# Forget gate moved into the attention stage, weight slots shared across stages, paired transposes, TensorE code without loops

## The reference, cut to what matters

```python
def even_layer(x, g_norm, w_in, b_f, w_out):          # x: (1, 1024, 1024)
    z = rms_norm(x, g_norm) @ w_in
    qa, ka, va, ga, fa, qb, kb, vb, gb = jnp.split(z, cuts, axis=-1)   # fa: 16 columns, the others 1024
    log_f = jax.nn.log_sigmoid(fa.astype(f32) + b_f.astype(f32))
    ya = forgetting_attention(hA(qa), hA(ka), hA(va), log_f)           # 16 heads of 64
    yb = dilated_attention(hB(qb), hB(kb), hB(vb))                     # 16 heads of 64
    y = jnp.concatenate([ya * jax.nn.silu(ga), yb * jax.nn.silu(gb)], axis=-1)
    return x + y @ w_out

# forgetting_attention: c = cumsum(log_f) over the sequence;
#   s = q.k * scale + c[t] - c[s], causal;  p = softmax(s);  o = p @ v
```

## Time and profile before

| | us |
|---|---|
| median of 3 runs | 4086.0 (4082.72 to 4088.43) |
| the profiled execution | 4084.06 |
| its span, first to last instruction | 4082.3 |
| PE busy | 3702.8 (91%) |
| DVE, ACT, POOL busy | 1756.0, 1314.9, 1336.3 |
| mean granted TensorE clock | 0.946 of full speed |

### The profile page before, as it was taken

How to read it: one execution, slowest core, us unless ns; L and a number is a source line. 1 busy time by engine, 2 the same in 40 slices (tenths; PEclk the granted TensorE clock), 3 DMA queues, 4 the chain that set the end, 5 groups by cost and what they waited for, 6 DMA issues and landing times. The chain is left out here.

```text
span 4082.3 us, 49492 instructions
## 1 busy us (share of the span) xinstructions
PE 3702.8 (91%) x17232; PEld 2952.5 (72%) x17232; DVE 1756.0 (43%) x3204; ACT 1314.9 (32%) x2399; POOL 1336.3 (33%) x795
## 2 busy tenths in 40 slices
PE   5987687879999996699999999997898999999797
PEld 4776554668888885588888888886677676868486
DVE  4666433353333335256565565655313323242432
ACT  3777132121001112265555655555101202020210
POOL 3210200233333330355555556664322121312032
PEclk8997799889999998899999999998999999999998
DMA  3000101221111101211311212310512020211141
GB/s 93 21 6 6 45 20 54 88 62 47 51 42 50 51 31 57 58 53 49 49 51 52 37 34 38 36 36 6 181 47 98 26 66 21 67 39 54 44 162 67
DMA packets 216104, 213.71 MB, mean 52 GB/s; under 512 B 12464, under 2 KB 174512, under 8 KB 216000
## 3 DMA queue, kind: packets, MB, share of 16 engines
q1 hardware_dynamic: 194160, 153.11, 14.4%
q10 hardware_dynamic: 21840, 59.25, 4.0%
HBM read 178.72 MB, written 33.62 MB: 52 GB/s over the span
## 5 line engine op out<-in xcount | busy, mean ns | idle before, releaser
L1138 POOL TENSOR_SCALAR even_probs<-even_probs,even_stat 128x128 f32<-128x128 f32 (+7 forms) x256 | 442.2, 1734 | 329.1 <-DVE even_stat L1515 329.1
L502 PE MATMUL ps<-all_u_hi,even_w_hi 128*128 128x512 f32 x1024 | 425.9, 416 | 25.1 <-POOL even_w_lo L1130 25.1
L506 PE MATMUL ps<-all_u_hi,even_w_lo 128*128 128x512 f32 x1024 | 403.0, 394 | 0.0
L505 PE MATMUL ps<-all_u_lo,even_w_hi 128*128 128x512 f32 x1024 | 400.3, 391 | 0.0
L455 POOL CAST odd_w_hi<-odd_w_raw 128x1024 fp32r<-128x1024 f32 x80 | 89.1, 1114 | 896.7 <-PE ps L502 688.1
L1520 DVE TENSOR_TENSOR even_probsT_lo<-ps,even_probsT_hi 128x512 fp32r<-128x512 f32 (+3 forms) x384 | 213.0, 555 | 280.8 <-ACT even_probsT_hi L1369 279.4
L502 PE MATMUL ps<-all_u_hi,odd_w_hi 128*128 128x512 f32 x768 | 305.5, 398 | 5.7 <-DVE ret_yT L2524 3.7
L505 PE MATMUL ps<-all_u_lo,odd_w_hi 128*128 128x512 f32 x768 | 303.4, 395 | 0.0
L506 PE MATMUL ps<-all_u_hi,odd_w_lo 128*128 128x512 f32 x768 | 303.1, 395 | 0.0
L1360 ACT ACTIVATE even_probs<-even_probs,even_stat 128x128 f32<-128x128 f32 (+7 forms) x256 | 199.0, 778 | 313.1 <-DVE even_stat L1509 313.1
L502 PEld LDWEIGHTS ps<-all_u_hi,even_w_hi 128*128 128x128 f32 x1024 | 194.2, 190 | 59.8 <-POOL even_w_lo L1130 25.5
(11 more groups left out here) (405 smaller groups left out, 8521.3 us busy)
## 6 DMA issues: line engine op xcount, KB each, us to landing
even_w_raw<-in_even_w_in_dram SPq DMA_DIRECT2D x64, 512.0 KB, 6.6
odd_w_raw<-in_odd_w_in_dram SPq DMA_DIRECT2D x48, 512.0 KB, 3.8
mlp_w_raw<-in_w_up_dram SPq DMA_DIRECT2D x32, 512.0 KB, 4.0
mlp_w_raw<-in_w_down_dram SPq DMA_DIRECT2D x32, 512.0 KB, 3.6
scratch_h<-residual SPq DMA_DIRECT2D x2, 4096.0 KB, 17.2
even_bias<-scratch_negc ACTq DMA_DIRECT2D x16, 512.0 KB, 6.4
scratch_yt<-even_yT ACTq DMA_DIRECT2D x32, 256.0 KB, 2.0
we_y_raw<-scratch_yt ACTq DMA_DIRECT2D x16, 512.0 KB, 4.3
```

Source lines behind the costliest of these rows:

```text
L502: ins = nc.tensor.matmul(dst, lh, rh, start=first, stop=False)
L505: nc.tensor.matmul(dst, lh, rl, start=False, stop=False)
L506: return nc.tensor.matmul(dst, ll, rh, start=False, stop=last)
L1138: nc.gpsimd.tensor_scalar(PB[g % 2][:, at], PB[g % 2][:, at], inv[:, s:s + 1], None, ALU.mult)\
```

## The change

1. **Forget gate.** `forget_stage` is gone. Its weight is loaded by SP first thing in the even stage into idle buffers, split by POOL, and its 48 matmuls stand on PE between the fourth and the fifth half product of the first pair (PSUM banks 6 and 7). Its chain on ACT and DVE stands between the copies; ACT itself issues the store of the sums, waits for it after the v copies, and only then issues the two bias reads of the first pair, which stood at the head of the stage before.
2. **Weight slots.** One pair of slots (`kept`) lives from "wo" to the end; the MLP adds two to them. `ne` now loads and splits two weights, the first pair's q and k. At its end the even stage loads and splits the first two slots of "we".
3. **Turns two by two.** In every even step PE issues the turns of n and n+1 one after the other, then the scores, eighths and weighing of n, then those of n+1. ACT and DVE copy both in the even step. The ring has 4 buffers. v is turned in steps 18 and 20 into half of a scores bank (`VBANK`), which is empty then.
4. **PE without loops.** PE's code of the even stage, the MLP, the out stages and the retention stage is written out. The other engines keep their loops.

```diff
@@ class Weights
-            self.raw = sb("w_raw", [P, slots, SEQ])
-            self.hi = sb("w_hi", [P, slots, SEQ], FR)
-            self.lo = sb("w_lo", [P, slots, SEQ], FR)
+            raw = sb("w_raw", [P, slots - old, SEQ])
+            hi = sb("w_hi", [P, slots - old, SEQ], FR)
+            lo = sb("w_lo", [P, slots - old, SEQ], FR)
+            self.raw, self.hi, self.lo = (Slots((parts.parts if base else []) + [t[:, s, :] for s in range(slots - old)])
...
@@ even_stage, SP
+                for dst, src in cols(weight, 4 * WIDTH)(f_raw):
+                    sp.dma_start(dst, src).then_inc(w_raw[4].sem, 16)
+                sp.dma_start(fb[:], b_f).then_inc(table_in.sem, 16)
+                for u in range(w.slots, per):
+                    w_load(sp, w, 0, per, u, cols(weight, bases[0][u]))
...
+                sp.wait_ge(w_lo.sem, w_lo.at(total * per + w.slots))
+                for u in range(w.slots):
+                    for dst, src in after(0, u)(w.raw[:, u, :]):
+                        sp.dma_start(dst, src).then_inc(w_raw[u].sem, 16)
@@ even_stage, PE
                 def attend(kind, nxt, it, left):
                     for n in range(NP):
-                        turn(it, n, nxt)
+                        if n % 2 == 0:
+                            turn(it, n, nxt)
+                            turn(it, n + 1, nxt)
                         if n in V_AT and nxt:
                             g = V_AT[n]
-                            if g == 0:
-
-                                pe.wait_ge(probs_out_dve.sem, probs_out_dve.at(NP * it + n))
-                            else:
+                            if g:
                                 pe.wait_ge(v_out_dve.sem, v_out_dve.at(2 * (it + 1) + 1))
-                            turn_v(it + 1, g, 1)
+                            turn_v(it + 1, g, VBANK)
...
                 for n in range(ND):
+                    if n == 4:
+                        forget()
...
-                each_pair(pe, attend)
+                each_pair(pe, attend, True)
+                w_open_pe(pe, w)
@@ even_stage, ACT
-                bias_in(0, 0)
-                bias_in(0, 1)
...
+                act.wait_ge(forget_dve.sem, forget_dve.at(4))
+                act.dma_start(NC, f_sum).then_inc(stored.sem, 16)
+                take_half(0, 6, 2)
+                take_half(0, 7, 3)
+                v_hi(0, 0, T[0])
+                v_hi(0, 1, T[1])
+                act.wait_ge(stored.sem, stored.at(16))
+                bias_in(0, 0)
+                bias_in(0, 1)
@@ even_stage, DVE
-                        probs_lo(it, n)
+                        if n % 2 == 0:
+                            probs_lo(it, n)
+                            probs_lo(it, n + 1)
@@ out_stage, mlp_stage, retention_stage (the same in each)
-                with pe.Fori(0, 2) as it:
+                for it in range(2):
@@ program
-        held, w = weights_for("forget", 1)
         norm_stage("ne", [(0, D, flat(even_norm))], resident=X, hi=UH, lo=UL, save=H,
-                   ahead=(w, 1, lambda it, u: cols(one(even_w_in), 4 * WIDTH)), opening=False)
-        forget_stage("forget", one(even_w_in), even_b_f.rearrange("a n -> n a"), w)
+                   ahead=(w, 4, pair_unit(one(even_w_in), even_bases[0])), opening=False)
...
-        out_stage("we", 2 * PAIRS, one(even_w_out), H, X, True, w, False)
+        out_stage("we", 2 * PAIRS, one(even_w_out), H, X, True, w, True)
```

222 lines of the change are left out of this document (114 added, 108 removed).

## The result

The changed kernel takes **4033.5 us** (median of 4 runs, 4031.9 to 4035.4) where the kernel before takes 4084.4 (median of 4). The ratio is 0.9876, with a 95% interval of 0.9864 to 0.9888. Of these 2.5 us, 1.6 come from the level that the forecast started from: it took 4086.0 for the kernel before, and with a fourth run that median is 4084.4. The profiled execution took 4034.2 us, its span 4032.5; the profiled span before was 4082.3.

A forecast was written before the change was run, and what follows sets the result against it. The kernel was taken to be bound by PE. Terms of 22.1 + 12 + 4.0 + 1.1 - 1.0 = 38.2 us off 4084.06 gave 4045.9, plus 1.9 for the runs' median: 4048 us, range 4036 to 4058.

The forecast's parts named there:

- Part 1: Forget gate and first weights, at the even stage's start: 22.1 us gained up to DVE's first scores.
- The second split: POOL's splitting of a second weight in `ne`: charged 1.0 us of delay to the product's start.
- The full exclusion: DVE and POOL excluding each other for a whole instruction in `ne`: DVE held up 2.4 us, not 1.0.
- Part 2: Joined turns and another bank for v, even stage: 0.8 us per pair, fifteen pairs, 12 us gained (6.5 to 20).
- Rival 2: Steps 18 and 19: waits come from busy ACT and DVE, so pairs stay as long; 4060; chance 0.08, late bias 0.03.
- Part 3: Start of "we" gains 4.0 us (3.5 to 4.4); last pair, with POOL's splits, costs 1.0 (-2.5 to +1).
- Part 4: PE without loops: 1.1 us gained (0 to 1.2) at three retention heads, nothing in the MLP.
- Rival 5: Jumps on PE cost more than seen: loop removal gives up to 9 us, 4040; included in the forecast's 0.68.
- Rival 4: Written-out PE code stalls on instruction fetch, some sixty stops; 4108 at 1 us each; chance 0.03.
- Rival 3: Even-stage pairs get longer as a second copy delays POOL's scaling; 4108 if 3.5 us later; chance 0.04.
- one of the signs of being wrong: Even stage: the turn of step 4 or 16 beginning to wait for POOL would show the forecast wrong.
- The range: Whole kernel: 4036 to 4058 us, from adding all terms' upper ends (49.7) or lower ends (27.6); chance 0.68.

The follow-up runs named there:

- part 2 undone: Changed kernel with turns one by one, three ring slots, and v turned into the probabilities' banks in steps 18 and 19: 4057.5 us.
- the three with late splits: Changed kernel with POOL's later weight splits moved to the next stage's start, 4027.2 us; two versions with further small edits, 4017.6 and 4021.9 us.

## Why the prediction missed

- **What bounds the kernel**: right. Every gain is idle time of PE or slow matmuls that went.
- **Part 1, 22.1 us**: right as a sum, by small errors that cancel. 23.9 from the product's start, less 2.2 for the longer way through `ne`, is 21.7. The bias read was as forecast, and issued 0.8 us earlier than I had counted. The second split was charged 1.0 us by the one stretched scaling of the earlier trace rows, and cost about 2 (the way through `ne` took 2.2 us more here, and 2.7 to 3.1 in the other traces with this order). The full exclusion that I had named beside it was the better price.
- **Part 2, 12 us: this step failed.** It says that "joining turns saves nothing by itself on PE", and it counts the whole 0.8 us of waiting in steps 18 and 19, which "comes from putting v and probabilities in the same bank", as gained once the bank is another. Joining gave 15.5 us in the stage, and the bank, on which all 12 rested, 6.4. (Together that is 1.5 us more than the 20.4 of the table. The kernel with part 2 undone is slower than the kernel before by that much, 0.8 of it in the last pair, on which part 3 has more.) Three things were wrong in it.
  - *The next wait.* The bank's waits were real, but behind them stood another. The weighing of step 18 waits for DVE, which is late by its gate product, and POOL's subtraction stretches this product from 1.22 to 2.30 us. Without the bank's waits PE stood there 0.38 us in a fox pair and 0.8 in a dilated one. Moving the product gave 9.9 us, and joining the turns takes this wait away too. Rival 2 named the right place (DVE has the gate product and the v copies in these steps), and then drew the wrong conclusion: the change did remove that wait. The row that I had for the product, is of the last pair, where no subtraction stood beside it.
  - *The sample.* 0.8 was read from one fox pair and multiplied by fifteen. The dilated pairs gain 1.45 each, the fox pairs 1.08. The wait is longer in the dilated ones: moving the gate product took 0.83 us from them and 0.45 from a fox pair.
  - *The rest.* Joins without the gate product in the way still give about 0.25 us per pair (gate moved with single turns 72.43 and 70.66, changed kernel 72.19 and 70.37), which I had at 0. That a turn's transposes cost the same wherever they stand is right; what falls is small waits ahead of single turns. Which of them, I did not separate.

  That 12 came as near to 18.1 as it did is luck: the term took too much from the bank and nothing from the joins.
- **Part 3, 4.0 and -1.0**: the start of "we" gave 2.0. The term was mis-sized because y does not lose the company of weight reads: the slots are free sooner, so the next two are issued beside y, and it lands in 5.5 us and not in 3.5. The last pair gained 2.4 us (3.4 to 3.7 in the other traces with all turns joined) where I had charged 1.0. The collision that I had charged for is real with single turns: with part 2 undone the gate product of the last pair takes 2.06 us beside POOL's subtraction where it took 1.22, PE's wait for `even_yT` behind it is 2.28 us in place of 1.44, and the pair takes 54.1 us in place of 53.3. With joined turns the product starts only 0.1 us ahead of the end of that subtraction, takes 1.22, and the wait is 0.83. So this miss too is the step on joined turns.
- **Part 4, 1.1 us**: right in size, 1.35 at the three heads. The 2.4 us of the whole stage lie within what its slow starts make of it from trace to trace. Rival 5 is dead: the MLP's 2972 matmuls take the same time with and without jumps. The Trainium skill, page "Runtime: NRT & Kernel Launch", section "Instruction fetch mechanics", says that a taken branch out of the current two pages waits for a fetch. No run here puts this to the test: with loops the MLP has 3 or 4 fetches of 16 KB in all, so its seven jumps do not fetch their target, and no stall shows where PE is busy. Rival 4 is dead too: instruction fetches went from 1.00 to 2.24 MB, and the pairs in straight code are as long as those in loops.
- **Not in the sum**: 2.7 us around the MLP. In `nm` the first weight landed later in the new order, POOL came behind DVE, and two scalings took 3.26 us in place of 5.42; further on the same collisions took part of it back. 1.8 us are the granted clock at the MLP's start.
- **Rival 3** exists in small: in dilated pairs PE waits about 0.3 us for POOL's scaling at the turn of step 16, against nothing before. It costs about 2 us in all, and is one of the signs of being wrong that the forecast names.
- **The range** reached to 4036, with every term at its upper end. The 18.1 us of the pairs lie inside the 6.5 to 20 of part 2, whose upper end was an allowance for waits that go elsewhere. What the ends did not hold was beside it: the last pair (+2.4, end +1), the retention stage (2.4, end 1.2), and the 2.7 us around the MLP, which had no term. Two of these three hold a share of the clock at a start, which I had given no spread. On the other side the start of "we" (2.0, low end 3.5) and the longer way through `ne` took some back.

## What to carry to other kernels

When a wait is to be removed, look for what the engine would wait for next, and count only the difference. Ahead of putting a wait down to a bank or a buffer, list the durations of each instruction form, stage by stage. A form with one mean here and nearly twice that mean there (1.22 and 2.30 us for the gate product, both in the trace of before) may be held up by another engine, and the instructions queued behind it explain waits that look like something else. Then either move it away from its rival or move the urgent work ahead of it. And read the per-period waiting from every kind of period before multiplying.

## What the hardware showed that was not expected

The same kernel's start from idle costs a different amount from one execution to another. The first hundred matmuls behind a norm or at a retention head took from 22.8 us to 26.2, at a granted clock that starts at 0.5 (1.2 GHz) and rises to 1.0 (2.4 GHz) sooner or later; at the MLP's start of the changed kernel it was 1.00 from the first one, and in the kernel before 0.50 for the first 1.9 us.

```profile
873.65 0.47 PE L516 MATMUL ps<-all_u_hi,kept_w_hi 128*128 128x512 f32 x1 [1.68 <-PEq L288]
873.96 0.39 PE L519 MATMUL ps<-all_u_lo,kept_w_hi 128*128 128x512 f32 x1
```

The kernel before, at the same place:

```profile
874.06 0.79 PE L502 MATMUL ps<-all_u_hi,mlp_w_hi 128*128 128x512 f32 x1 [1.91 <-PEq L284]
874.65 0.63 PE L505 MATMUL ps<-all_u_lo,mlp_w_hi 128*128 128x512 f32 x1
```

In the second trace of the changed kernel this start was slow again, 24.4 us for the hundred where the first had 22.8. Nine of the traces are of kernels with the same code up to there: seven started fast, two slow. The kernel before, the one with loops and the three with late splits, one trace each, all started slow. So the 1.8 us may belong to the change in most executions; these traces do not show why. A shorter hole ahead of a retention head did not bring a shorter head: with idle times of 0.78 us the heads' first hundred matmuls took between 24.7 and 26.2 us, with 1.23 us between 25.4 and 25.7. The Trainium skill, page "TensorE: Matmul & The Clock Gate", Part 1, says that the number of slow matmuls at a start varies from run to run; the traces agree. With some eight such starts, and the 10 us by which the stretch up to "wo" differs between traces, a sum of terms for this kernel cannot be better than a few us for one execution.
